# The first three layer norms of a two-block transformer kernel computed by halves of the tokens

## The chip, the cores and the metric

One NeuronCore of one Trainium2 chip runs the whole program; the metric is device microseconds of one execution, lower is better. The engines are TensorE (PE, with PEld for its weight loads), VectorE (DVE), ScalarE (ACT), GpSimd (POOL) and SyncE (SP), which only issues transfers here.

## The reference

x is 512 tokens by 1024 features, fp32. Two blocks run one after the other, each of two layers. Only the first block has the norms of this case:

```python
def layer_norm(x, g, b):
    mu = mean(x, -1); var = mean(square(x - mu), -1)
    return (x - mu) * rsqrt(var + 1e-5) * g + b

for i in range(2):
    mix = s5_mixer(h) if i == 0 else stick_breaking_mixer(h)   # end in h @ w_out, o @ w_o
    h = layer_norm(ALPHA * h + mix, ...)                       # norm 0, norm 2
    h = layer_norm(ALPHA * h + swiglu_ffn(h), ...)             # norm 1, norm 3
```

ALPHA is 4 ** 0.25. swiglu_ffn is (silu(g) * u) @ w_down with (g, u) = split(h @ w_gu), hidden width 2816. The second block (gated attention, a convolutional feed-forward, rms norms 4 to 7) follows and is not changed.

## The kernel before

**Layout.** Features lie on the 128 partitions and tokens on the free axis, so a tensor of 1024 features is 8 chunks of 128x512. `res` (residual) holds h in fp32. Each operand of a dense product is split into a high part rounded to fp32r and a low part, the rest: `xhi`, `xlo` for the input, `whi`, `wlo` for the weights. A product takes three matmuls for each k-chunk: hi*hi, lo*hi, hi*lo.

**Stages.** The program is a list of dense stages in order: glu, ssm_out, gu0, down0, q, k, v, w_o, gu1, down1, ev_u and so on. Weights come in tiles of 128x2048, two buffers (half 0 and half 1) of each of `w_stage`, `w_hi`, `w_lo`. SP loads `w_stage`; ACT casts it to `w_hi` (L1562) once PE has done with the tile before in that buffer; DVE subtracts to make `w_lo` (L2207). ssm_out and w_o have four tiles and 8 output chunks of 24 matmuls each, gathered in banks 0 to 3 of PSUM. In the last pass PE does chunks 4 and 5 from tile half 0 (L975 to L977), then chunks 6 and 7 from tile half 1 (L845 to L847). down0 has one output chunk for each pair of tiles, 66 matmuls of 11 k-chunks a tile. The stage behind a norm (gu0, q, gu1) begins with 48 matmuls of two output chunks on its tile half 0, for each k both chunks, and each k waits for `x_ready` of that k; then 48 on tile half 1.

**Norm n of 0, 1, 2, as it is before.** DVE writes the residual chunk `res` (L2252) and its square (L2263) when PE has done the chunk. POOL sums the chunks and the squares into `acc` (L573) and `acc_sq` (L575), one by one, up to chunk 6, and then makes `w_lo` of tile half 1 of the next stage (L559, `split_last`). PE forms the sums over partitions as matmuls with a matrix of ones: `acc` (L1062), chunk 7 (L1064), `acc_sq` (L1065), the square of chunk 7 (L1067), 512 tokens wide, fp32. ACT squares the mean (L1609), DVE subtracts for the variance (L2336), ACT does Ln and Exp for 1/sqrt (L1611, L1613). Then for each of 8 chunks DVE subtracts the mean (`centre`, L2339) and multiplies (L2350), ACT writes `xhi` (L1619) and `res` (L1620) with gain and bias, and DVE writes `xlo` (L2343), which raises `x_ready`. All engines take their instructions in the order written; all waits are semaphore counts written by hand.

**Halved stages that exist before.** ev_out, cdown0 and od_out (norms 5, 6, 7, rms) already do their last output chunks by halves of the tokens: first tokens 0 to 255 of the last chunks, then tokens 256 to 511 (`halved_units`, `halved_unit`, L857 to L859), with the sums of the first half between (`half_mean_square`, L869, L872). The next stage starts with `first_units_by_halves` (L926 to L928): for each weight tile, first 8 k-chunks of tokens 0 to 255, then of 256 to 511, each waiting for `x_ready` of that k and half; between k 1 and k 2 of the first half stand the sums of the second. There DVE has two operations for a chunk and half, and `w_lo` of tile half 1 is made by POOL.

## Time and profile before

| | |
|---|---|
| median of 3 runs | 2556.41 us (2554.3 to 2556.71) |
| profiled execution, its own time | 2554.76 us |
| span of its trace | 2553.0 us |
| granted TensorE clock, mean | 0.981 |
| busy: PE, DVE, ACT, POOL | 96%, 48%, 32%, 12% |

The time of the execution is 1.76 us more than the span, from the first instruction to the last. A row of the timeline gives start, duration and instruction, and in brackets how long its engine sat idle before it and what ended that. A matmul's recorded duration is longer than the distance to the next one, since matmuls are pipelined; distances between starts are what counts. The granted clock is 1.00 at 2.4 GHz and 0.50 at 1.2 GHz.

### The profile page before, as it was taken

How to read it: one execution, taken by the hardware profiler on the slowest of the kernel's cores; microseconds unless marked ns; L12 is line 12 of the kernel's file. 1: busy time of each engine (PE TensorE's matmuls, PEld its weight loads, DVE VectorE, ACT ScalarE, POOL GpSimd, SP SyncE). 2: the span in 40 equal slices, each digit the busy share in tenths (PEclk: the TensorE clock that was granted, in tenths of full speed). 3: DMA queues.
4: the chain of work that ended last, by engine and by line, in shares of the span. 5: the costliest groups of instructions: out<-in, count | busy, mean ns of one | idle time of the engine just before them, and what ended most of it. 6: DMA issues, size and time to landing. Idle time of an engine off the chain costs nothing.

```text
span 2553.0 us, 32215 instructions
## 1 busy us (share of the span) xinstructions
PE 2459.4 (96%) x12941; PEld 2017.4 (79%) x12941; DVE 1233.3 (48%) x1618; ACT 824.9 (32%) x923; POOL 304.7 (12%) x213
## 2 busy tenths in 40 slices
PE   7699999999999989999989989999999999999999
PEld 6587788887897668888858758888889986988887
DVE  8835433345435564333544464555434445644432
ACT  5422322223225523222243363333323243432222
POOL 6503000004000040000221013000023001100000
PEclk8899999999999989999999989999999999999999
DMA  2432232233320013322342211323233221233232
GB/s 54 92 103 92 83 98 91 77 102 95 99 86 14 11 56 99 99 93 80 91 121 67 67 34 50 108 92 98 85 93 105 83 83 50 83 99 99 84 91 90
DMA packets 254438, 210.30 MB, mean 82 GB/s; under 512 B 7156, under 2 KB 252298, under 8 KB 254250
## 3 DMA queue, kind: packets, MB, share of 16 engines
q1 hardware_dynamic: 250682, 205.99, 26.2%
q8 instruction: 102, 1.67, 0.3%
q0 software_dynamic: 976, 1.74, 0.3%
q10 hardware_dynamic: 2656, 0.72, 0.1%
q14 instruction: 22, 0.18, 0.0%
HBM read 203.97 MB, written 2.10 MB: 81 GB/s over the span
## 4 chain that ended last, share of the span: by engine, by line
PE 89%; DVE 7%; ACT 2%; POOL 1%; issue 1%; DMA 0%; SPq 0%; DVEq 0%; POOLq 0%; ACTq 0%
PE psum L845 14%; PE psum L847 14%; PE psum L846 14%; PE psum L975 9%; PE psum L976 9%; PE psum L977 9%; PE psum L1088 2%; PE psum L1089 2%; PE psum L1090 2%; POOL tmp_a L575 1%; PE psum L1120 1%; PE psum L1138 1%; PE psum L926 1%; PE psum L927 1%; PE psum L928 1%
## 5 line engine op out<-in xcount | busy, mean ns | idle before, releaser
L1562 ACT CAST w_hi<-w_stage 128x2048 fp32r<-128x2048 f32 x209 | 400.4, 1916 | 1341.2 <-PE psum L847 714.5
L2207 DVE TENSOR_TENSOR w_lo<-w_stage,w_hi 128x2048 fp32r<-128x2048 f32 x202 | 473.8, 2345 | 634.5 <-ACT w_hi L1562 634.4
L975 PE MATMUL psum<-x_hi,w_hi 128*128 128x512 f32 x864 | 341.1, 395 | 19.9 <-DVE x_lo L2343 16.1
L845 PE MATMUL psum<-x_hi,w_hi 128*128 128x512 f32 x888 | 345.9, 390 | 0.0
L846 PE MATMUL psum<-x_lo,w_hi 128*128 128x512 f32 x888 | 345.5, 389 | 0.0
L847 PE MATMUL psum<-x_hi,w_lo 128*128 128x512 f32 x888 | 345.5, 389 | 0.0
L976 PE MATMUL psum<-x_lo,w_hi 128*128 128x512 f32 x864 | 339.7, 393 | 0.0
L977 PE MATMUL psum<-x_hi,w_lo 128*128 128x512 f32 x864 | 339.3, 393 | 0.0
L845 PE MATMUL psum<-hidden_hi,w_hi 128*128 128x512 f32 x746 | 291.4, 391 | 0.8 <-DVE w_lo L2207 0.8
L847 PE MATMUL psum<-hidden_hi,w_lo 128*128 128x512 f32 x746 | 290.3, 389 | 0.0
L846 PE MATMUL psum<-hidden_lo,w_hi 128*128 128x512 f32 x746 | 290.2, 389 | 0.0
L975 PEld LDWEIGHTS psum<-x_hi,w_hi 128*128 128x128 f32 x864 | 164.4, 190 | 58.4 <-issue 23.5
L845 PEld LDWEIGHTS psum<-x_hi,w_hi 128*128 128x128 f32 x888 | 166.7, 188 | 35.2 <-issue 0.7
L847 PEld LDWEIGHTS psum<-x_hi,w_lo 128*128 128x128 f32 x888 | 166.7, 188 | 34.7
L846 PEld LDWEIGHTS psum<-x_lo,w_hi 128*128 128x128 f32 x888 | 166.7, 188 | 34.4
L977 PEld LDWEIGHTS psum<-x_hi,w_lo 128*128 128x128 f32 x864 | 164.3, 190 | 34.7
L976 PEld LDWEIGHTS psum<-x_lo,w_hi 128*128 128x128 f32 x864 | 164.5, 190 | 34.0
L845 PEld LDWEIGHTS psum<-hidden_hi,w_hi 128*128 128x128 f32 x746 | 140.0, 188 | 30.8 <-issue 2.1
L846 PEld LDWEIGHTS psum<-hidden_lo,w_hi 128*128 128x128 f32 x746 | 140.0, 188 | 29.5 <-issue 0.5
L847 PEld LDWEIGHTS psum<-hidden_hi,w_lo 128*128 128x128 f32 x746 | 140.0, 188 | 29.2
L565 POOL TENSOR_TENSOR tmp_a<-residual 128x512 f32<-128x512 f32 x4 | 7.2, 1793 | 945.3 <-DVE residual L2252 831.0
L1088 PE MATMUL psum<-w_hi,x_hi 128*128 128x256 f32 x384 | 109.6, 285 | 0.8 <-ACT qk_rstd L1780 0.8
(436 smaller groups left out, 3437.9 us busy)
## 6 DMA issues: line engine op xcount, KB each, us to landing
w_stage<-in_ffn_w_gu_dram SPq DMA_DIRECT2D x44, 1024.0 KB, 5.1
w_stage<-in_ffn_w_down_dram SPq DMA_DIRECT2D x64, 704.0 KB, 4.6
w_stage<-in_ffn_w_gate_dram SPq DMA_DIRECT2D x22, 1024.0 KB, 5.2
w_stage<-in_ffn_w_up_dram SPq DMA_DIRECT2D x22, 1024.0 KB, 5.4
w_stage<-in_sb_w_qkv_dram SPq DMA_DIRECT2D x12, 1024.0 KB, 5.1
w_stage<-in_od_w_in_dram SPq DMA_DIRECT2D x12, 1024.0 KB, 5.3
w_stage<-in_ev_w_in_dram SPq DMA_DIRECT2D x10, 1024.0 KB, 5.1
w_stage<-in_ssm_w_glu_dram SPq DMA_DIRECT2D x8, 1024.0 KB, 5.5
```

The source lines that it names most:

```text
L575: sum_link(nc.gpsimd.tensor_tensor(acc_sq, acc_sq, dev_slot[c], ALU.add))
L845: nc.tensor.matmul(dst, hi, x_hi, start=(start and k == 0), stop=False)
L846: nc.tensor.matmul(dst, hi, x_lo, start=False, stop=False)
L847: mm = nc.tensor.matmul(dst, lo, x_hi, start=False, stop=(stop and k == kn - 1))
L975: nc.tensor.matmul(dst[u], hi, x_hi, start=(k == order[0]), stop=False)
L976: nc.tensor.matmul(dst[u], hi, x_lo, start=False, stop=False)
L977: mm = nc.tensor.matmul(dst[u], lo, x_hi, start=False, stop=(k == order[-1]))
L1088: nc.tensor.matmul(dst, hi, wh[:, k, :], start=(k == 0), stop=False)
L1089: nc.tensor.matmul(dst, hi, wl[:, k, :], start=False, stop=False)
L1090: mm = nc.tensor.matmul(dst, lo, wh[:, k, :], start=False, stop=(k == DC - 1))
L1562: nc.scalar.copy(whi[:, half, :], wst[:, half, :]).then_inc(whi_done, 1)
L2207: V.tensor_tensor(wlo[:, half, :], wst[:, half, :], whi[:, half, :].bitcast(F32), ALU.subtract).then_inc(wlo_done, 1)
```

## The change

Norms 0, 1 and 2 are treated by halves of the tokens. ssm_out, down0 and w_o join the halved stages (chunks 6 and 7 by halves for norms 0 and 2, chunk 7 for norm 1); gu0, q and gu1 start with `first_units_by_halves`. POOL sums only the chunks ahead of the halved ones (to chunk 5, for norm 1 to chunk 6). PE takes the halved chunks and their squares into the sums by matmuls of 256 tokens: three and three for each half (two and two for norm 1), where there were four of 512. ACT and DVE do the norm as 16 steps of 128x256 where there were 8 of 128x512. POOL's `split_last` falls away for these norms; ACT's cast of tile half 1 moves into its norm loop (behind step 9), and DVE makes `w_lo` of it behind its step 10. For norm 1 the cast and subtraction of tile half 0 of the next stage stand behind step 1 too. `xlo` is written by DVE, as before. Norms 3 to 7 keep their work and get new counts.

```diff
-HALVED_LAST = {"ev_out": 2, "cdown0": 1, "od_out": 2}
+HALVED_LAST = {"ssm_out": 2, "down0": 1, "w_o": 2, "ev_out": 2, "cdown0": 1, "od_out": 2}
...
-            return (DC - 1,) if n == 6 else (DC - 2, DC - 1)
+            return (DC - 1,) if n in (1, 6) else (DC - 2, DC - 1)
...
+        mean_half, ln_rstd_half = (bank[5][:, 0:HALF], bank[4][:, HALF:SEQ]), (bank[6][:, 0:HALF], bank[7][:, HALF:SEQ])
...
                 pool.wait_ge(shift_done, n + 1)
-                for c in range(1, DC - 1):
+                for c in range(1, DC - 1 if n == 3 else halved_chunks(n)[0]):
...
-                split_last(n)
+                if n == 3:
+                    split_last(n)
...
                 if h == 0:
                     pe.wait_ge(acc_link, acc_count(n - 1) + 2 * last[0] - 1)
-                else:
+                if n < 3:
+                    nc.tensor.matmul(mean_half[h], ones_mean[:, :], acc[:, tokens], start=True, stop=False)
+                    for c in last:
+                        pe.wait_ge(evac_done, half_done(n, h, c))
+                        mm = nc.tensor.matmul(mean_half[h], ones_mean[:, :], res[:, c, tokens], start=False, stop=(c == last[-1]))
+                    mm.then_inc(ln_sums, 1)
+                    nc.tensor.matmul(ln_rstd_half[h], ones_mean[:, :], acc_sq[:, tokens], start=True, stop=False)
+                    for c in last:
+                        pe.wait_ge(dev_sq, squares_before(n) + last[0] + h * len(last) + (c - last[0]) + 1)
+                        mm = nc.tensor.matmul(ln_rstd_half[h], ones_mean[:, :], dev_slot[c][:, tokens], start=False,
+                                              stop=(c == last[-1]))
+                    mm.then_inc(ln_sums, 1)
+                    return
+                if h == 1:
                     pe.wait_ge(act_link, link_count(n) + 2)
...
                 elif name == "ssm_out":
-                    feature_stage(name, hhi, hlo, lambda k: (hid_ready, DC + k + 1), 0)
-                    norm(0)
+                    feature_stage(name, hhi, hlo, lambda k: (hid_ready, DC + k + 1), 0, norm_out=0)
                 elif name == "gu0":
-                    feature_stage(name, xhi, xlo, lambda k: (x_ready, 1 * DC + k + 1))
+                    feature_stage(name, xhi, xlo, lambda k: (x_ready, x_count(1)), norm_in=0)
...
+            def layer_norm_by_halves(n, affine):
...
+                mean_square_of(0)
+                rstd_of(0)
+                for m in range(2 * DC):
+                    tokens, c = TOKEN_HALVES[m // DC], m % DC
+                    act.wait_ge(ln_n, done + m + 1)
+                    g, b = (prm[:, col + c:col + c + 1] for col in affine)
+                    nc.scalar.activation(xhi[:, c, tokens], res[:, c, tokens], ACT.Identity, bias=b, scale=g).then_inc(ln_hi, 1)
+                    nc.scalar.activation(res[:, c, tokens], res[:, c, tokens], ACT.Identity, bias=b, scale=g).then_inc(ln_a, 1)
+                    if m == 1 and n == 1:
+                        split(st.it0 + st.iters, 0, st.part1 - 1)
+                    if m == 4:
+                        mean_square_of(1)
+                    if m == 5:
+                        rstd_of(1)
+                    if m == DC + 1:
+                        split(st.it0 + st.iters, 1, st.part1)
...
+            def norm_by_halves(n):
...
+                def residual_half(c, h):
...
+                    dve.wait_ge(part_done, parts)
+                    dve.wait_ge(ln_shifted, n * DC + c + 1)
+                    V.scalar_tensor_tensor(res[:, c, tokens], res[:, c, tokens], ALPHA, of[:, tokens], ALU.mult,
+                                           ALU.add).then_inc(evac_done, 1)
+                    dve.wait_ge(evac_done, half_done(n, h, c))
...
+                    V.tensor_tensor(dev_slot[c][:, tokens], res[:, c, tokens], res[:, c, tokens], ALU.mult).then_inc(dev_sq, 1)
...
+                for c in last:
+                    residual_half(c, 0)
+                variance_of(0)
+                centre(0)
+                centre(1)
+                if n != 1:
+                    residual_half(DC - 2, 1)
+                dve.wait_ge(act_link, link_count(n) + 2)
+                for m in range(DC):
+                    scale(m)
+                    if m + 2 < DC:
+                        centre(m + 2)
+                    if m == 1 and n == 1:
+                        split(st.it0 + st.iters, 0)
+                    if m == (2 if n == 1 else 1):
+                        residual_half(DC - 1, 1)
+                    if m > 1:
+                        low_part(m - 2)
+                    if m == 5:
+                        variance_of(1)
+                centre(DC)
+                low_part(DC - 2)
+                centre(DC + 1)
+                low_part(DC - 1)
+                dve.wait_ge(act_link, link_count(n) + 4)
+                for m in range(DC, 2 * DC):
+                    scale(m)
+                    if m + 2 < 2 * DC:
+                        centre(m + 2)
+                    if m > DC + 1:
+                        low_part(m - 2)
+                    if m == DC + 2:
+                        split(st.it0 + st.iters, 1)
+                low_part(2 * DC - 2)
+                low_part(2 * DC - 1)
```

down0 and w_o, q and gu1 are changed like ssm_out and gu0. `variance_of`, `centre`, `scale` and `low_part` are the DVE operations of before on 256 tokens, each with its wait.

## Rows read from the trace of the kernel before

The columns of the waits are: engine and line that waited, what it waited for, us in total, times, longest. Those of a stretch are: its ends, its length, busy us and instructions of PE, PEld, DVE, ACT and POOL, granted clock, DMA share, GB/s.

**Rows 1.** The page: the chain that ended last, share of the span by engine.
```profile
PE 89%; DVE 7%; ACT 2%; POOL 1%; issue 1%; DMA 0%; SPq 0%; DVEq 0%; POOLq 0%; ACTq 0%
```

**Rows 2.** Waits of PE over the whole span.
```profile
PE psum L975 <- DVE x_lo L2343: 16.1, 3, 5.5
...
PE psum L1062 <- POOL tmp_a L575: 5.7, 2, 2.9
```

**Rows 3.** Timeline of PE around the first norm: start us, us, instruction, idle before.
```profile
249.25 0.39 PE L847 MATMUL psum<-hidden_hi,w_lo 128*128 128x512 f32 x1
...
249.93 0.39 PE L847 MATMUL psum<-hidden_hi,w_lo 128*128 128x512 f32 x1
...
253.15 1.13 PE L1062 MATMUL psum<-tmp_a,ones_mean 128*128 128x512 f32 x2 [2.83 <-POOL tmp_a L575]
...
262.19 0.77 PE L975 MATMUL psum<-x_hi,w_hi 128*128 128x512 f32 x1 [5.34 <-DVE x_lo L2343]
...
276.01 0.39 PE L845 MATMUL psum<-x_hi,w_hi 128*128 128x512 f32 x1
```

**Rows 4.** Timeline of PE around the second and third norm.
```profile
625.56 0.39 PE L847 MATMUL psum<-hidden_hi,w_lo 128*128 128x512 f32 x1
...
648.49 0.39 PE L845 MATMUL psum<-x_hi,w_hi 128*128 128x512 f32 x1
...
938.25 0.39 PE L847 MATMUL psum<-hidden_hi,w_lo 128*128 128x512 f32 x1
...
967.02 0.39 PE L845 MATMUL psum<-x_hi,w_hi 128*128 128x512 f32 x1
```

**Rows 5.** Stretches behind idle time of PE: busy us (count), granted clock, DMA.
```profile
262.20:268.30 6.10, 6.10 (x14) 4.75 (x15) 6.10 (x11) 5.02 (x7) 0.00 (x0) 0.50 0.01 3
...
941.50:948.20 6.70, 6.68 (x8) 2.52 (x8) 0.00 (x0) 0.60 (x1) 4.50 (x1) 0.55 0.00 0
```

**Rows 6.** Timeline of PE in a stage already halved, ev_out into conv0.
```profile
1569.92 0.28 PE L857 MATMUL psum<-x_hi,w_hi 128*128 128x256 f32 x1
...
1577.47 0.60 PE L869 MATMUL psum<-tmp_a,ones_mean 128*128 128x256 f32 x2
...
1578.88 0.28 PE L858 MATMUL psum<-x_lo,w_hi 128*128 128x256 f32 x1
...
1608.20 0.40 PE L975 MATMUL psum<-x_hi,w_hi 128*128 128x512 f32 x1
```

**Rows 7.** Timeline of DVE: first norm, and two half-width steps of ev_out.
```profile
242.50 3.37 DVE L2207 TENSOR_TENSOR w_lo<-w_stage,w_hi 128x2048 fp32r<-128x2048 f32 x1
...
256.96 0.69 DVE L2336 TENSOR_TENSOR tmp_c<-psum,tmp_c 128x512 f32<-128x512 f32 x1 [4.98 <-PE psum L1067]
...
259.07 0.69 DVE L2350 TENSOR_TENSOR residual<-residual,psum 128x512 f32<-128x512 f32 x1 [0.23 <-ACT psum L1613]
...
263.16 0.69 DVE L2343 TENSOR_TENSOR x_lo<-residual,x_hi 128x512 fp32r<-128x512 f32 x1
...
264.95 0.69 DVE L2343 TENSOR_TENSOR x_lo<-residual,x_hi 128x512 fp32r<-128x512 f32 x1
...
1582.02 0.41 DVE L2476 TENSOR_TENSOR residual<-residual,psum 128x256 f32<-128x256 f32 x1
...
1582.35 0.48 DVE L2485 SCALAR_TENSOR_TENSOR psum<-residual,params,psum 128x256 f32<-128x256 f32 x1
```

**Rows 8.** Timeline of POOL: its last sum of chunk 5, first norm.
```profile
248.79 1.28 POOL L575 TENSOR_TENSOR tmp_a<-tmp_a,squares 128x512 f32<-128x512 f32 x1
```

**Rows 9.** Groups by form: line, engine, shapes, count | busy, mean ns | idle.
```profile
L1562 ACT CAST w_hi<-w_stage 128x2048 fp32r<-128x2048 f32 x209 | 400.4, 1916 | 1341.2 <-PE psum L847 714.5 <-PE psum L977 526.3 <-PE psum L1090 80.8
...
L1620 ACT ACTIVATE residual<-residual,params 128x512 f32<-128x512 f32 x32 | 25.7, 804 | 1.1 <-DVE residual L2350 1.1
...
L1646 ACT ACTIVATE squares<-residual 128x256 f32<-128x256 f32 x10 | 4.2, 419 | 16.2 <-DVE residual L2476 16.2
...
L2207 DVE TENSOR_TENSOR w_lo<-w_stage,w_hi 128x2048 fp32r<-128x2048 f32 x202 | 473.8, 2345 | 634.5 <-ACT w_hi L1562 634.4
```

More of the change, by code:

```diff
@@ L1626, in layer_norm, with mean_square_of, rstd_of @@
                         nc.scalar.activation(sq[:, (c - 1) % 2, :], res[:, c - 1, :], ACT.Square).then_inc(ln_sq, 1)
+            def layer_norm_by_halves(n, affine):
+                st, last = ST[norm_stage[n]], halved_chunks(n)
+                done = n * 2 * DC
+                def mean_square_of(h):
+                    act.wait_ge(ln_sums, 4 * n + 2 * h + 1)
+                    nc.scalar.activation(mean_sq[:, TOKEN_HALVES[h]], mean_half[h], ACT.Square).then_inc(ln_m2, 1)
+                def rstd_of(h):
+                    tokens = TOKEN_HALVES[h]
+                    act.wait_ge(ln_var, 2 * n + h + 1)
+                    nc.scalar.activation(rstd_ln[:, tokens], variance[:, tokens], ACT.Ln, bias=eps_ln[:, 0:1]).then_inc(act_link, 1)
+                    act.wait_ge(act_link, link_count(n) + 2 * h + 1)
+                    nc.scalar.activation(ln_rstd_half[h], rstd_ln[:, tokens], ACT.Exp, scale=-0.5).then_inc(act_link, 1)
+                mean_square_of(0)
[14 more added lines that the diff above has]
+                        split(st.it0 + st.iters, 1, st.part1)
             def rms_norm(n):
@@ L2317, in down_stage @@
                     shift(n)
-                    for c in range(looped, DC):
+                    for c in range(looped, DC if n == 3 else DC - 1):
                         unit(c - c % 2, c % 2, c < DC - 1, True)
@@ L2355, in norm, with variance_of, centre, scale @@
                 pass_split(n)
-                if n < 3:
-                    low(DC - 1)
+            def norm_by_halves(n):
+                st, last = ST[norm_stage[n]], halved_chunks(n)
+                before = n * 2 * DC
+                def residual_half(c, h):
+                    tokens = TOKEN_HALVES[h]
+                    if n == 1:
+                        parts, of = st.part1 - 2 * (1 - h), bank[1 + h]
+                    else:
+                        parts, of = st.part1 - 4 + 2 * h + (c - last[0]) + 1, bank[2 + c - last[0]]
+                    dve.wait_ge(part_done, parts)
[3 more added lines that the diff above has]
+                    dve.wait_ge(evac_done, half_done(n, h, c))
+                    if c == DC - 1:
+                        dve.wait_ge(acc_link, acc_count(n - 1) + 3)
+                    V.tensor_tensor(dev_slot[c][:, tokens], res[:, c, tokens], res[:, c, tokens], ALU.mult).then_inc(dev_sq, 1)
+                def variance_of(h):
+                    tokens = TOKEN_HALVES[h]
+                    dve.wait_ge(ln_m2, 2 * n + h + 1)
+                    dve.wait_ge(ln_sums, 4 * n + 2 * h + 2)
+                    V.tensor_tensor(variance[:, tokens], ln_rstd_half[h], mean_sq[:, tokens], ALU.subtract).then_inc(ln_var, 1)
+                def centre(m):
+                    tokens, c = TOKEN_HALVES[m // DC], m % DC
+                    V.tensor_tensor(res[:, c, tokens], res[:, c, tokens], mean_half[m // DC], ALU.subtract).then_inc(ln_xc, 1)
+                def scale(m):
+                    tokens, c = TOKEN_HALVES[m // DC], m % DC
+                    dve.wait_ge(ln_xc, before + m + 1)
+                    V.tensor_tensor(res[:, c, tokens], res[:, c, tokens], ln_rstd_half[m // DC], ALU.mult).then_inc(ln_n, 1)
+                def low_part(m):
+                    tokens, c = TOKEN_HALVES[m // DC], m % DC
+                    dve.wait_ge(ln_a, before + m + 1)
+                    V.tensor_tensor(xlo[:, c, tokens], res[:, c, tokens], xhi[:, c, tokens].bitcast(F32),
+                                    ALU.subtract).then_inc(x_ready, 1)
+                for c in last:
[5 more added lines that the diff above has]
+                    residual_half(DC - 2, 1)
+                dve.wait_ge(act_link, link_count(n) + 2)
+                for m in range(DC):
[25 more added lines that the diff above has]
+                low_part(2 * DC - 1)
@@ L2740, in _ @@
                     down_stage(name, 1)
-                    norm(1)
+                    norm_by_halves(1)
                 elif name == "q":
```

81 lines of the change are left out of this document (37 added, 44 removed).

## Prediction

> **What bounds the kernel now.** I read the page's chain first: PE sets the end for 89% of the span [rows 1], so time is won or lost only where PE stands idle, runs at half clock, or does more matmuls. The list of PE's waits then says where: three waits for `xlo`, 16.1 us, one behind each of norms 0, 1 and 2, and two for POOL's sums, 5.7 us, at norms 0 and 2 [rows 2]. The timelines of PE give the whole price of a norm: from the start of the last dense matmul before it to the start of the 49th behind it, less 49 matmuls at their distance. That distance is (249.93 - 249.25) / 3 = 0.227 us [rows 3], so 49 are 11.1 us. Norm 0 costs 276.01 - 249.93 - 11.1 = 15.0 us [rows 3]; norm 1 costs 648.49 - 625.56 - 11.1 = 11.8 and norm 2 costs 967.02 - 938.25 - 11.1 = 17.7 [rows 4]. Together 44.5 us. In these lie spells of half clock: behind the 5.34 us of idle time of norm 0 the clock is 0.50 for 6.1 us [rows 3, 5], and 6.7 us after 941.5, behind the second wait for POOL, it is 0.55 [rows 5].
>
> The question is what the same stretches cost by halves. Each engine takes its instructions in order, so I lay them out, with these prices.
>
> **Prices of the pieces.**
> - A dense matmul of 256 tokens: (1577.47 - 1569.92) / 63 = 0.120 us [rows 6], against 0.113 for half of 0.227.
> - A sum of 256 tokens in fp32: three of them and the first step behind took 1578.88 - 1577.47 = 1.41 us [rows 6]; less one dense matmul that is 0.37 each and 0.18 once. Six are 2.4 us, four 1.7.
> - DVE at 128x256: 1582.35 - 1582.02 = 0.33 us from start to start [rows 7]. At 512 a loop step of three operations took 264.95 - 263.16 = 1.79, or 0.60 each [rows 7]. So a step of centre, scale, low is 1.0 us by halves, 16 steps 16 us against 14.3.
> - ACT at 128x256 with gain and bias is in no row. It lies between 0.42, a Square of that shape, and 0.80, the same operation at 512 [rows 9]. I take the middle, 0.61 or 0.50 from start to start (0.09 overlap as on DVE); the low end gives 0.42 from start to start and the high end 0.71. A step has two, so 1.0 us: ACT and DVE are level.
> - Cast of a weight tile on ACT 1.92, subtraction on DVE 2.35 [rows 9], less where nothing contends; I use 2.25.
> - From the variance to the first scale took 259.07 - 256.96 = 2.1 us at 512 [rows 7]; at 256 I take 1.4 (between 1.05, half, and 2.1).
>
> The Trainium skill ("VectorE: DVE Perf Modes", section on the TRN2 errata for SBUF-source operations) says that each instruction pays a fixed cost and advises tiles of 512 elements or more. The trace agrees, 0.33 against half of 0.60; without that cost 16 steps would be 14.3 us, with it 16. It speaks against this change, by 1.7 us a norm on DVE.
>
> **Norm 0, laid out.** Chunk 6 starts at 249.93 - 47 x 0.227 = 239.28. Its first half is 24 x 0.120 = 2.88 us, to 242.16, chunk 7's to 245.04. For the second half of chunk 6 PE needs the bank evacuated, but DVE is in a weight subtraction from 242.50 to 245.87 [rows 7]. Evacuation ends at 246.29: PE waits 1.3. Fifteen matmuls later, at 248.1, it wants POOL's sums to chunk 5; the last of them ends at 248.79 + 1.28 = 250.07 [rows 8]. PE waits 2.0. POOL's list ahead of that is the one of before, only chunk 6 (two sums) and its weight subtraction go. Sums to 252.5, the other 33 matmuls to 256.5.
>
> DVE starts the variance at 252.6 and scale 0 at 254.6, behind the evacuation and square of chunk 6's second half. Behind scale 1 it stands before the evacuation of chunk 7's second half, which PE finishes at 256.5; then come both operations, scale 2, centre 4, and only then low 0, done at 258.6. PE waits 2.1. From there `xlo` comes at 1.0 us a step, where PE needs 6 x 0.120 = 0.72. PE does k 0 and k 1, then the second sums (2.4), which cover some steps; DVE waits 1.3 for them before its second variance. Step 7 is there at 266.7, step 8 at 269.0.
>
> **The wait that decides.** Behind low 8 DVE must subtract the weights of tile half 1. ACT casts them only behind its step 9: cast from 269.05 to 270.96, DVE idle 2.1 us, subtraction to 273.2. Queued behind it are scale 11 and low 9, and PE's k 9 waits for low 9: done at 274.25, PE idle 4.5 us at k 9. The cast and POOL's L559 were in nobody's way before; POOL took that subtraction in 4.5 us beside the norm. Low 10 to 15 follow to 279.2, k 15 ends at 279.9, and tile half 1 takes 96 x 0.120 = 11.5: 291.45. Before it was 276.01 + 48 x 0.227 = 286.9 [rows 3]. Norm 0: **+4.6 us**.
>
> **Norm 1.** Chunk 7 starts at 625.56 - 65 x 0.227 = 610.8. First half 66 x 0.120, to 618.8, 12 matmuls, four sums at 620.2 (POOL has nothing left there), second half done at 628.3. Scale 0 at 623.4, scale 1, and now the cast of tile half 0, which ACT reaches at 625.8: DVE idle 3.1, subtraction 627.8 to 630.0. Then scale 2, chunk 7's evacuation and square, low 0 at 631.8; PE idle 3.5. Step 8 at 641.6, the second cast and subtraction as in norm 0 (PE idle 4.5), low 15 at 651.8, end of tile half 1 at 664.0. Before: 648.49 + 10.9 = 659.4 [rows 4]. **+4.7 us**.
>
> **Norm 2** has the list of norm 0; its end lies 291.45 - 249.93 = 41.5 behind the last dense matmul: 979.8, against 967.02 + 10.9 = 977.9 [rows 4]. **+1.9 us**, better than norm 0 because the sums of before ran at half clock there. Sum at full clock: **+11.2 us**.
>
> SP's load of the next tile for half 1 can start at 273.2, when `w_stage` is free, and its cast is wanted at 291, so it stays hidden (before, the free point was POOL's and DVE's mark behind the norm loop). The three norms are the only places changed; the new counts of norms 3 to 7 move nothing.
>
> **The clock.** Half clock stands behind the wait of 5.34 us [rows 3, 5] and behind the second wait for POOL, of 2.9 us [rows 2]: eight passes of the sums in 6.7 us there [rows 5]. Behind the first, of 2.83 us, it does not: two passes in 1.13 us [rows 3]. The new wait at k 9 is 4.5 us, so I take half clock behind it for 5.1 us, 24 dense matmuls at 0.213. They need 1.28 us a k against DVE's 1.0, and what PE falls behind is partly caught up at 0.72: +1.6 us for each norm, +4.9. If the clock falls at the waits of 2 us as well, the sums take double, which delays DVE too: then the norms cost 11.7, 10.4 and 9.0 more than before, +31.
>
> The Trainium skill ("TensorE: Matmul & The Clock Gate", Part 1) says that idleness brings half clock and sustained work releases it. The trace agrees [rows 5]; by the rule the case with fallen clock is the likelier, as taken.
>
> **The forecast.** 11.2 + 4.9 = 16.1 us more. The sum is made against the profiled execution, 2554.76 us (span 2553.0 and 1.76 around it): 2570.9. The runs' median is 1.65 above it, so 2572.4.
>
> **Rivals.**
> 1. The same without fallen clock, +11.2: 2567.6. For it: the waits are shorter than 5.34. Chance 0.22; the forecast 0.42.
> 2. Half clock at the short waits too, +31: 2587. Chance 0.13. For it the 2.86 us row, against it the 2.83 us one.
> 3. The casts and subtractions of tile half 1 cost PE nothing, because the second half of x is not waited for: then my layout gives +1.0, +1.1, -1.7, together +0.4: 2556.8, no difference. Against it stands the order on DVE. Chance 0.12.
> 4. **Faster:** the layer norm by halves costs PE what the rms norm by halves costs in ev_out and conv0. There it took 1608.20 - 1569.92 = 38.3 us [rows 6] for 144 matmuls of 512, 32.7 us: 5.6 lost. With three more sums a half, 2.2 us, that is 7.8 a norm, 23.4 for three against 44.5: -21.1, 2535.3. For it: PE had hardly a wait for `xlo` there. Against it: DVE had two operations a step and no weight subtraction in the norm. It decides where a norm loses less than (44.5 - 5.1) / 3 = 13.1 us; my layout has 19.6 in norms 0 and 2, 16.5 in norm 1. Chance 0.11.
>
> 0.2% is 5.1 us, about what a measurement of this kernel can tell from no change. Slower: forecast, rivals 1 and 2, 0.77. Same: 0.12. Faster: 0.11. The likeliest case alone has 2563 to 2579: the low end is ACT at 0.42 and DVE at 0.30 a step, which takes 4.5 off the +11.2, with part of the clock loss; the high end is ACT at 0.54 and DVE at 0.36, +3.5, and a little more clock. The range for 8 in 10 goes from rival 3, 2556, to 2583, which leaves out rival 4 and most of rival 2.
>
> **What the profile after would show.** PE idle about 4.5 us once in each of gu0, q and gu1, inside the first tile, waiting for `xlo`, with DVE's `w_lo` before it, itself waiting for ACT's `w_hi`: the step that carries the result. PE waiting some 2 us for POOL's `tmp_a` in ssm_out and w_o, and 2 to 3.5 us before the first matmul of the next stage. `xlo` steps 1.0 us apart. Half clock behind the long wait. ACT's operations at 0.6 us or less. The prediction is wrong if the three stretches, from the last 512-wide matmul to the end of the next stage's first two tiles, together are not longer than before (in norm 0: 36.9 us from 249.93), or if PE reaches the second half without waiting.

## The result, and the profile after

The changed kernel takes 2575.59 us in the median (2573.39 to 2578.39, 4 runs) where the kernel before took 2555.51 on the same chip: a ratio of 1.0079, 95% interval 1.0063 to 1.0095. It is slower by 0.8%. The forecast was 2572.4, range 2556 to 2583. The profiled execution took 2577.76 us (span 2575.9), 23.0 more than the one of before.

The list of PE's waits after the change, over the whole span. The two lines of [rows 2] that it replaces are gone.

```profile
PE psum L946 <- DVE x_lo L2438: 24.6, 9, 4.3
...
PE psum L875 <- POOL tmp_a L581: 3.2, 2, 1.6
...
PE psum L864 <- DVE residual L2413: 2.1, 2, 1.1
...
PE psum L864 <- DVE w_lo L2255: 1.4, 2, 1.0
```

Nine waits for `xlo` where there were three, 24.6 us instead of 16.1. PE's timeline at norm 0, after the change (columns as in [rows 3]):

```profile
243.81 0.28 PE L864 MATMUL psum<-hidden_hi,w_hi 128*128 128x256 f32 x1
...
250.79 0.39 PE L864 MATMUL psum<-hidden_hi,w_hi 128*128 128x256 f32 x1 [1.07 <-DVE residual L2413]
...
254.42 0.70 PE L875 MATMUL psum<-tmp_a,ones_mean 128*128 128x256 f32 x2 [1.57 <-POOL tmp_a L581]
...
263.30 0.36 PE L946 MATMUL psum<-x_hi,w_hi 128*128 128x256 f32 x1 [2.06 <-DVE x_lo L2438]
...
265.01 0.60 PE L875 MATMUL psum<-tmp_a,ones_mean 128*128 128x256 f32 x2
...
274.10 0.39 PE L946 MATMUL psum<-x_hi,w_hi 128*128 128x256 f32 x1 [1.34 <-DVE x_lo L2438]
...
279.34 0.58 PE L946 MATMUL psum<-x_hi,w_hi 128*128 128x256 f32 x1 [4.26 <-DVE x_lo L2438]
...
297.37 0.40 PE L995 MATMUL psum<-x_hi,w_hi 128*128 128x512 f32 x1
```

Four small waits, the last of them (1.34 us) at k 8, then the long one at k 9. What made it stands in the timelines of ACT and DVE in the same stretch:

```profile
274.07 1.89 ACT L1579 CAST w_hi<-w_stage 128x2048 fp32r<-128x2048 f32 x1
...
273.63 0.42 DVE L2438 TENSOR_TENSOR x_lo<-residual,x_hi 128x256 fp32r<-128x256 f32 x1
275.99 2.29 DVE L2255 TENSOR_TENSOR w_lo<-w_stage,w_hi 128x2048 fp32r<-128x2048 f32 x1 [1.95 <-ACT w_hi L1579]
...
278.87 0.42 DVE L2438 TENSOR_TENSOR x_lo<-residual,x_hi 128x256 fp32r<-128x256 f32 x1
```

Low 8 ends at 274.05 and low 9 starts at 278.87: between them DVE is idle 1.95 us for ACT's cast, then subtracts weights for 2.2 and does a scale and a centre.

The yardstick below is a stretch that holds a whole norm: from the first half-width matmul of the stage ahead of it to the first 512-wide matmul of the third weight tile behind it. After the change the three are 297.37 - 243.81 = 53.56, 57.66 and 53.43 us. Before, the same work began 47, 65 and 47 matmuls ahead of the start rows and ended 48 behind the end rows of [rows 3, 4]: 47.61, 48.54 and 50.31, together 146.46. The windows of the kernel after, cut at these points, say where all the time went (columns as in [rows 5]):

```profile
0.00:243.80 243.80, 207.24 (x1921) 179.58 (x1922) 157.09 (x342) 85.76 (x99) 85.11 (x82) 0.90 0.32 85
243.80:297.40 53.60, 43.19 (x314) 40.97 (x313) 32.76 (x67) 26.72 (x44) 10.18 (x6) 0.94 0.18 60
297.40:621.30 323.90, 323.49 (x1426) 267.17 (x1425) 133.65 (x120) 76.14 (x55) 21.73 (x11) 1.00 0.30 93
621.30:679.00 57.70, 47.40 (x342) 45.57 (x341) 31.23 (x63) 26.35 (x42) 5.42 (x4) 0.91 0.26 83
679.00:947.20 268.20, 268.20 (x1540) 209.28 (x1539) 135.45 (x195) 96.43 (x111) 11.59 (x6) 1.00 0.16 52
947.20:1000.70 53.50, 43.09 (x314) 40.85 (x313) 32.79 (x67) 26.72 (x44) 10.20 (x6) 0.94 0.18 60
1000.70:2575.90 1575.20, 1542.45 (x7586) 1272.42 (x7584) 724.66 (x854) 499.81 (x585) 140.65 (x93) 0.99 0.28 85
```

Before, cut in the same way:

```profile
0.00:239.30 239.30, 200.85 (x1922) 173.77 (x1923) 157.08 (x342) 85.63 (x99) 85.15 (x82) 0.94 0.32 86
...
286.90:610.80 323.90, 323.48 (x1425) 267.27 (x1424) 132.01 (x117) 76.36 (x55) 21.74 (x11) 1.00 0.30 93
...
659.40:927.60 268.20, 268.20 (x1540) 209.28 (x1539) 134.96 (x194) 96.64 (x111) 11.62 (x6) 1.00 0.16 52
...
977.90:2553.00 1575.10, 1542.20 (x7585) 1272.30 (x7583) 723.02 (x851) 500.88 (x585) 140.72 (x93) 0.99 0.28 85
```

The parts between and behind the norms are equal to 0.1 us. The norms cost 18.2 us more (6.0, 9.1 and 3.1; 146.46 became 164.65). The start-up, which the change does not touch, took 4.5 us more in this execution, at a mean granted clock of 0.90 instead of 0.94. In the profiled executions of all kernels below it ends anywhere between 239.27 and 244.28 us. So a single time is uncertain by some 5 us, and the sum of the three stretches is the sharper measure of a norm. It comes from one execution of each kernel and has a spread of its own: norm 1, which e5_front and e6_order below leave as it is, took 57.58 and 58.85 us in them against 57.66 here.

### The profile page after: what moved, and what is told of

Same layout as the page of the kernel before. It is cut to its first block, busy times and chain, and to the rows that moved or that the text cites. A ratio compares the mean times of both kernels' runs of the same rounds, so it can differ in the third digit from the quotient of the medians.

```text
span 2575.9 us, 33325 instructions
## 1 busy us (share of the span) xinstructions
PE 2475.0 (96%) x13431; PEld 2055.8 (80%) x13431; DVE 1247.6 (48%) x1703; ACT 837.9 (33%) x980; POOL 284.9 (11%) x206
## 4 chain that ended last, share of the span: by engine, by line
PE 88%; DVE 7%; ACT 2%; POOL 1%; issue 1%; DMA 0%; SPq 0%; DVEq 0%; POOLq 0%; ACTq 0%
PE psum L852 14%; PE psum L853 14%; PE psum L854 14%; PE psum L995 8%; PE psum L997 8%; PE psum L996 8%; PE psum L1108 2%; PE psum L1109 2%; PE psum L1110 2%; PE psum L946 2%; PE psum L947 1%; PE psum L948 1%; ACT w_hi L1579 1%; DVE w_lo L2255 1%; POOL tmp_a L581 1%
## 5 line engine op out<-in xcount | busy, mean ns | idle before, releaser
L852 PE MATMUL psum<-x_hi,w_hi 128*128 128x512 f32 x840 | 327.2, 390 | 0.0
L853 PE MATMUL psum<-x_lo,w_hi 128*128 128x512 f32 x840 | 326.9, 389 | 0.0
L854 PE MATMUL psum<-x_hi,w_lo 128*128 128x512 f32 x840 | 326.8, 389 | 0.0
L995 PE MATMUL psum<-x_hi,w_hi 128*128 128x512 f32 x816 | 318.6, 390 | 3.7 <-DVE x_lo L2580 3.7
L997 PE MATMUL psum<-x_hi,w_lo 128*128 128x512 f32 x816 | 318.2, 390 | 0.0
L996 PE MATMUL psum<-x_lo,w_hi 128*128 128x512 f32 x816 | 318.0, 390 | 0.0
L852 PE MATMUL psum<-hidden_hi,w_hi 128*128 128x512 f32 x692 | 270.4, 391 | 0.8 <-DVE w_lo L2255 0.8
L854 PE MATMUL psum<-hidden_hi,w_lo 128*128 128x512 f32 x692 | 269.3, 389 | 0.0
L853 PE MATMUL psum<-hidden_lo,w_hi 128*128 128x512 f32 x692 | 269.3, 389 | 0.0
L852 PEld LDWEIGHTS psum<-x_hi,w_hi 128*128 128x128 f32 x840 | 157.7, 188 | 33.4 <-issue 0.7
L854 PEld LDWEIGHTS psum<-x_hi,w_lo 128*128 128x128 f32 x840 | 157.7, 188 | 32.9
L853 PEld LDWEIGHTS psum<-x_lo,w_hi 128*128 128x128 f32 x840 | 157.7, 188 | 32.5
L995 PEld LDWEIGHTS psum<-x_hi,w_hi 128*128 128x128 f32 x816 | 153.6, 188 | 36.3 <-issue 4.7
L997 PEld LDWEIGHTS psum<-x_hi,w_lo 128*128 128x128 f32 x816 | 153.5, 188 | 32.1
L996 PEld LDWEIGHTS psum<-x_lo,w_hi 128*128 128x128 f32 x816 | 153.6, 188 | 31.6
L946 PE MATMUL psum<-x_hi,w_hi 128*128 128x256 f32 x384 | 116.4, 303 | 26.1 <-DVE x_lo L2438 24.6
```

What stands on the lines that cost most here:

```text
L852: nc.tensor.matmul(dst, hi, x_hi, start=(start and k == 0), stop=False)
L853: nc.tensor.matmul(dst, hi, x_lo, start=False, stop=False)
L854: mm = nc.tensor.matmul(dst, lo, x_hi, start=False, stop=(stop and k == kn - 1))
L946: nc.tensor.matmul(dst, hi, xh[:, k, tokens], start=(k == 0), stop=False)
L995: nc.tensor.matmul(dst[u], hi, x_hi, start=(k == order[0]), stop=False)
L996: nc.tensor.matmul(dst[u], hi, x_lo, start=False, stop=False)
```

## The experiments

Eleven further kernels ran. The results in one table; the change of the stretches is against 146.46, that of the time is the ratio less 1, times 2555.

| kernel | stretches, us | sum | against before | ratio (95% interval) | as time |
|---|---|---|---|---|---|
| changed kernel | 53.56, 57.66, 53.43 | 164.65 | +18.2 | 1.0079 (1.0063 to 1.0095) | +20.2 |
| e1_late | 52.04, 58.13, 54.70 | 164.87 | +18.4 | 1.0072 (1.0058 to 1.0085) | +18.4 |
| e2_pool | 56.84, 59.35, 55.24 | 171.43 | +25.0 | 1.0097 (1.0082 to 1.0112) | +24.8 |
| e3_early | 50.85, 53.91, 50.86 | 155.62 | +9.2 | 1.0033 (1.0020 to 1.0046) | +8.4 |
| e4_fill | 52.75, 57.15, 54.10 | 164.00 | +17.5 | 1.0074 (1.0061 to 1.0087) | +18.9 |
| e5_front | 51.55, 57.58, 53.09 | 162.22 | +15.8 | 1.0064 (1.0050 to 1.0078) | +16.4 |
| e6_order | 53.28, 58.85, 52.81 | 164.94 | +18.5 | 1.0069 (1.0056 to 1.0083) | +17.6 |
| e7_cast0 | 53.47, 53.98, 53.49 | 160.94 | +14.5 | 1.0068 (1.0054 to 1.0082) | +17.4 |
| e8_all | 48.52, 52.27, 48.51 | 149.30 | +2.8 | 1.0012 (1.0003 to 1.0021) | +3.1 |
| e9_whi_first | 50.48, 53.03, 50.72 | 154.23 | +7.8 | 1.0037 (1.0023 to 1.0051) | +9.5 |
| e10_last | 45.84, 48.96, 45.85 | 140.65 | -5.8 | 0.9973 (0.9964 to 0.9983) | -6.9 |
| e11_cast_mid | 46.37, 50.11, 46.36 | 142.84 | -3.6 | 0.9988 (0.9979 to 0.9997) | -3.1 |

The two measures agree within 3 us everywhere, so what a kernel gains or loses it does in these stretches.

**e1_late: the splits of tile half 1 behind the last step.**

```diff
 # ACT, layer_norm_by_halves: out of the loop
-                    if m == DC + 1:
-                        split(st.it0 + st.iters, 1, st.part1)
+                split(st.it0 + st.iters, 1, st.part1)
 # DVE, norm_by_halves
-                    if m == DC + 2:
-                        split(st.it0 + st.iters, 1)
                 low_part(2 * DC - 2)
                 low_part(2 * DC - 1)
+                split(st.it0 + st.iters, 1)
```

> ACT's cast of tile half 1 and DVE's subtraction both stand behind step 15 of the norm, in all three norms; nothing else differs from the changed kernel. Theory (the cast and the subtraction cost PE because they stand ahead of low 9): the 4.3 us waits of PE for x_lo at k 9 vanish and low 15 is done at 281.1 in norm 0 instead of 284.1, but the cast then starts at 280.7, the subtraction ends at 284.8, and PE, through with k 15 at 281.9, waits some 2.9 us for w_lo: next 512-wide matmul at 296.3 instead of 297.4, so 1.1 us a norm less, and 2 us less where the clock then stays at 1.00: in all 3 to 6 us less than the changed kernel (2575.6). Rival (the second half of x is not what PE waits for, the splits are costless once they are behind it): the whole wait and its clock go, 5.9 us a norm, 17.7 in all, 2558. Rival (where they stand makes no difference, only their length counts): no change.

Median 2574.91 us, ratio 1.0072. The wait at k 9 is gone in all three norms and a wait for `w_lo` stands ahead of tile half 1 instead. PE in e1_late, norm 0, at k 9 and at the start of tile half 1:

```profile
271.52 0.38 PE L946 MATMUL psum<-x_hi,w_hi 128*128 128x256 f32 x1
...
280.67 0.38 PE L946 MATMUL psum<-x_hi,w_hi 128*128 128x256 f32 x1 [2.68 <-DVE w_lo L2254]
```

The long wait was for the queue position of the split, as the theory says, and moving it to the end only makes PE wait for the split itself: 2.7 us against the 2.9 expected, and 1.5 us won in norm 0. In norms 1 and 2 the stretches grew by 0.5 and 1.3, so the 3 to 6 us expected in all did not come. That is clock: behind the same wait of 2.7 us PE took 11.6 us for tile half 1 in norm 0, 13.1 in norm 1 and 14.3 in norm 2, at a granted clock of 1.00, 0.87 and 0.79. Taken whole, this kernel can't be told from the changed one.

**e2_pool: POOL makes that `w_lo` again. ACT's cast stays behind its step 9.**

```diff
-                if n == 3:
-                    split_last(n)
+                split_last(n)
...
 # DVE: the split behind step 10 goes
                 low_part(2 * DC - 1)
+                pass_split(n)
```

> POOL makes w_lo of tile half 1 again in the three norms, as in the kernel before; ACT's cast stays behind its step 9; DVE passes the count behind low 15. Theory, DVE's queue alone: DVE has no hole at step 10 beyond ACT's cast, so of the 4.3 us wait at k 9 some 1.5 us are left, at k 10, low 15 comes at 282.4 instead of 284.1, and the next 512-wide matmul 2.8 us earlier than in the changed kernel in norm 0; 8 us less in three norms, 2567, somewhat less with the half clock gone. Rival (contention): DVE's operations with two operands in SBUF take 1.05 us instead of 0.42 while POOL runs its sums (squares of 256 tokens at 250.77 and 252.19 in the profile after), so about four lows beside POOL's 4.5 us take 0.7 us more each, and POOL itself takes longer: the gain is eaten, 0 to 2 us in all. Rival (the wait at k 9 was no more than a shift of work): no change and PE waits the same 4.3 us elsewhere.

Median 2581.24 us, ratio 1.0097: 6.8 us more in the stretches than the changed kernel, worse than even the contention rival gave. POOL, then DVE in e2_pool:

```profile
274.98 4.50 POOL L565 TENSOR_TENSOR w_lo<-w_stage,w_hi 128x2048 fp32r<-128x2048 f32 x1 [23.16 <-ACT w_hi L1578]
```

```profile
275.87 3.90 DVE L2437 TENSOR_TENSOR x_lo<-residual,x_hi 128x256 fp32r<-128x256 f32 x1 [1.28 <-ACT residual L1665]
279.69 0.41 DVE L2432 TENSOR_TENSOR residual<-residual,psum 128x256 f32<-128x256 f32 x1
```

One `low_part`, 0.42 us elsewhere, takes 3.90 us: it starts inside POOL's subtraction and ends at 279.77, 0.3 us behind POOL's end at 279.48. It is not slowed in proportion, it stands until POOL has finished, and the whole norm behind it. Norms 1 and 2 show the same, with 3.91 us each. The four lows of 0.7 us more each in the expectation had the wrong form; it is one low that pays for nearly all of POOL's instruction. The Trainium skill ("SBUF — State Buffer", section "SBUF: two separate sides") says that a DVE operation with two SBUF inputs and a GpSimd operation take a common port pair by turns, whole instruction by whole instruction. The trace agrees, by the end of the low 0.3 us behind POOL's. Not all of the 6.8 us is this: ahead of k 8, where the kernels do the same work, e2_pool lost 1.4 us in norm 0 and 1.1 in norm 1 to half clock around the second sums. From k 8 on it lost 1.8, 0.6 and 1.8 us, together 4.2.

Before the change POOL's subtraction ran from 253.17 to 257.68 in norm 0, ahead of the first low (261.35). That place is gone: in the changed kernel PE uses the old weights of tile half 1 until its matmul at 260.95, and low 0 starts at 262.73. That an earlier cast would not have helped POOL is argued from these times; no such kernel was run.

**e3_early: the splits where ACT and DVE wait for the second sums anyway.**

```diff
 # ACT
                     if m == 4:
+                        split(st.it0 + st.iters, 1, st.part1)
                         mean_square_of(1)
 # DVE
                     if m == 5:
+                        split(st.it0 + st.iters, 1)
                         variance_of(1)
 # the splits behind ACT's step 9 and DVE's step 10 go
```

> ACT's cast of tile half 1 stands ahead of its square of the second mean (behind step 4), DVE's subtraction ahead of its second variance (behind step 5): both fall into the time in which ACT (1.1 us) and DVE (1.7 us) wait for PE's second sums. Theory: the 4.3 us wait at k 9 goes in all three norms, the second variance comes 0.5 to 0.9 us later, low 15 is done about 280.7 in norm 0 instead of 284.1, and the next 512-wide matmul comes 4.4 us earlier; 13 us less in all, about 2562, still 6 to 7 us above the kernel before. Rival (PE needs a total of DVE work, its place is indifferent): the wait moves to k 4 or k 8 with the same 4 us, 0 to 2 us less. Rival (layer norm by halves loses only through this wait and its clock): 18 us less, level with the kernel before at 2556.

Median 2564.49 us, ratio 1.0033: 9.0 us less in the stretches than the changed kernel (13 expected), 11.1 less in time. The largest of the three waits for `xlo` in each norm is gone. Ahead of it two things happen that the expectation did not have. PE and DVE in e3_early, norm 0, and then norm 2:

```profile
261.45 0.36 PE L946 MATMUL psum<-x_hi,w_hi 128*128 128x256 f32 x1 [2.06 <-DVE x_lo L2437]
...
263.83 1.05 PE L875 MATMUL psum<-tmp_a,ones_mean 128*128 128x256 f32 x2
...
266.93 0.47 PE L946 MATMUL psum<-x_hi,w_hi 128*128 128x256 f32 x1
...
268.92 0.39 PE L946 MATMUL psum<-x_hi,w_hi 128*128 128x256 f32 x1 [0.22 <-DVE x_lo L2437]
```

```profile
267.79 0.42 DVE L2423 TENSOR_TENSOR tmp_c<-psum,tmp_c 128x256 f32<-128x256 f32 x1
```

```profile
958.38 0.36 PE L946 MATMUL psum<-x_hi,w_hi 128*128 128x256 f32 x1 [2.06 <-DVE x_lo L2437]
...
962.51 0.47 PE L946 MATMUL psum<-x_hi,w_hi 128*128 128x256 f32 x1
...
965.86 0.38 PE L946 MATMUL psum<-x_hi,w_hi 128*128 128x256 f32 x1 [1.57 <-DVE x_lo L2437]
```

First, behind the same wait of 2.06 us the same 12 matmuls and six sums take 5.5 us in norm 0, at half clock, and 4.1 in norm 2. The difference costs nothing here: PE only waits 0.22 us at k 4 instead of 1.57, and k 8 starts 32.0 us behind the start of the stretch in both, which take 50.85 and 50.86 us. Second, DVE's place was not free. The subtraction waits 1.28 us for ACT's cast, and the second variance (L2423) starts 25.8 us behind the start of the stretch in both norms, against 24.1 in the changed kernel: 1.75 later, where 0.5 to 0.9 was expected. This is what holds k 4 and k 8. Low 15 of norm 0 is done 1.9 us earlier in the stretch than in the changed kernel, where 3.4 was expected. About 1 us of the 1.5 missing is the late variance; the rest was not followed. So the rival is right in part: some of the long wait moved to k 4.

**e4_fill: 33 matmuls of no use ahead of the wait at k 9.**

```diff
+                            if n < 3 and pair == 0 and h == 1 and k == 0:
+                                for _ in range(33):
+                                    nc.tensor.matmul(bank[5][:, 0:HALF], whi[:, 0, 0:P], xh[:, 0, 0:HALF], start=True, stop=True)
```

> Ahead of PE's wait at k 9 of the second half, in the three norms, PE does 33 additional matmuls of 256 tokens into a bank that nothing reads any more (4.0 us of the 4.3 us wait). No other work changes. Theory (half clock behind the wait costs 1.6 us or more a norm): granted clock 1.00 behind k 9 in all three norms, next 512-wide matmul 1.5 to 2 us earlier in each, 5 us less in all, 2571. Rival 1 of the prediction (the clock costs nothing, DVE sets the pace there): the clock is 1.00 and the time is that of the changed kernel. Rival: the filler only delays PE where the wait is shorter than 4 us; some us more.

Median 2574.46 us, ratio 1.0074. From k 9 to the end of the stretch (PE and the windows of e4_fill, norm 0):

```profile
276.90 0.39 PE L946 MATMUL psum<-x_hi,w_hi 128*128 128x256 f32 x1 [0.30 <-DVE x_lo L2441]
...
294.13 0.40 PE L998 MATMUL psum<-x_hi,w_hi 128*128 128x512 f32 x1
```

```profile
276.90:294.10 17.20, 17.16 (x138) 16.75 (x139) 6.44 (x14) 8.56 (x13) 0.00 (x0) 1.00 0.38 123
```

and the same stretch of the changed kernel:

```profile
279.30:297.30 18.00, 17.96 (x138) 17.96 (x139) 6.46 (x13) 8.59 (x13) 0.00 (x0) 0.91 0.36 118
```

At full clock it takes 17.23 us, in all three norms. In the changed kernel it took 18.03, 18.56 and 17.90. Half clock behind the long wait cost 0.8, 1.3 and 0.7 us, together 2.8. The forecast had 1.6 for each and this expectation 1.5 to 2. Of these 2.8 us the sum shows 0.6, because ahead of k 9 norms 1 and 2 were 0.8 and 1.3 us longer this time (the part that the filler does not touch; the second sums and first matmuls ran at half clock there).

**e5_front, e6_order, e7_cast0: three smaller places, each alone** (the last two edits in short form).

```diff
 # e5_front, DVE out_stage, and norm_by_halves for norms 0 and 2
-                    elif c % 2 == 1 and c < DC - 1:
+                    elif c % 2 == 1 and (c < 5 or n not in (0, 2)):
                         split(st.it0 + 1 + c // 4, c % 4 // 2)
...
                 for c in last:
                     residual_half(c, 0)
+                if n != 1:
+                    split(st.it0 + st.iters, 0)
                 variance_of(0)
 # e6_order, DVE, norms 0 and 2
-                    if m == 1: residual_half(DC - 1, 1)
+                    if m == 2: low_part(0); residual_half(DC - 1, 1); low_part(1)
 # e7_cast0, norm 1: ACT, then DVE
-                    if m == 1: split(half 0)
+                    if m == 0: split(half 0)
-                    if m == 1: split(half 0)
-                    if m == 2: residual_half(DC - 1, 1); low_part(0)
+                    if m == 2: low_part(0); split(half 0); residual_half(DC - 1, 1); low_part(1)
```

> For norms 0 and 2 DVE's subtraction for tile half 0 of the next stage stands behind the two evacuations of the first halves (chunks 6 and 7) instead of ahead of them; all else as in the changed kernel. Theory: PE's 1.07 us wait for the bank goes, and POOL's sum beside that subtraction (3.21 us long there, 1.3 to 1.7 elsewhere) is shortened, so that the sums of the first half end about 1.4 us earlier in norm 0 (256.93 before) and everything behind them too: 53.56 becomes about 52.1 us from the first half-width matmul to the next 512-wide one, the same in norm 2 (53.43); 3 us less in all. Rival: POOL's last sums are beside the moved subtraction now and end as late as before; PE only waits 1.07 longer at the sums, no gain. Norm 1 stays at 57.7.

51.55 us in norm 0, 2.0 less than in the changed kernel (1.4 expected), 0.3 less in norm 2. PE's wait for the bank is gone and the one for POOL is 1.00 us instead of 1.57, in both. The rival is out in norm 0; in norm 2 the first matmul of the next stage came 1.9 us earlier too, but the k 9 matmul only 0.6. Between them PE ran at half clock behind the wait of 2.06 us: the second sums took 3.0 us instead of 2.4. In total time none of e5_front, e6_order and e7_cast0 can be told from the changed kernel, so all three are judged by their stretches.

> For norms 0 and 2 low 0 stands ahead of, and low 1 directly behind, the evacuation and square of the second half of chunk 7, which itself stands behind step 2 instead of step 1. Theory (PE's 2.06 us wait ahead of the next stage is for an xlo that stands behind an evacuation that itself waits for PE): the wait shrinks to about 0.3 us, the second sums start 1.6 us earlier, DVE's idle 1.7 us ahead of its second variance goes, and the next 512-wide matmul comes 1.6 us earlier in norms 0 and 2; 3 us less in all. The wait of 4.3 us at k 9 stays as long as it is. Rival (a chain elsewhere sets the end): the time moves into the wait at k 9 or at k 8 and the stretch stays 53.5 us.

The theory was right on the wait and wrong on the gain. PE's wait ahead of the next stage fell from 2.06 to 0.51 us and k 9 came 34.1 us behind the start of the stretch instead of 35.5. But the stretch is only 0.3 us shorter in norm 0. PE, then the windows, of e6_order:

```profile
275.47 0.58 PE L946 MATMUL psum<-x_hi,w_hi 128*128 128x256 f32 x1 [4.26 <-DVE x_lo L2438]
...
294.66 0.40 PE L995 MATMUL psum<-x_hi,w_hi 128*128 128x512 f32 x1
```

```profile
275.00:281.00 6.00, 5.53 (x26) 5.53 (x27) 4.60 (x14) 5.98 (x11) 0.00 (x0) 0.50 0.56 178
```

From k 9 on it took 19.2 us where full clock takes 17.2: six microseconds at half clock, where the changed kernel had a mean of 0.66 over 4.7. Of the 1.4 us won 1.2 went to the clock. Norm 2 gained 0.6. Norm 1, which the edit leaves alone, took 1.2 more in this execution, so the sum shows no gain.

> Norm 1 alone: ACT casts tile half 0 of the next stage behind its step 0 instead of step 1, and DVE's order is step 2, low 0, the subtraction, the evacuation of chunk 7's second half, low 1. Theory: the subtraction ends 1.0 us earlier and low 0 and low 1 no longer stand behind it with the evacuation and a step between, so that the first matmul of q comes some 19.5 us behind the first half-width matmul of down0 instead of 22.55, PE's wait of 3.66 us falls to about 0.6, and the clock does not fall behind it (the four second sums then take 1.7 us, not 2.3): the stretch of norm 1 is 53.3 to 54.7 us instead of 57.66, 3 to 4.4 us less in all. Rival (the clock does not hang on this wait): 3 us less at most, sums still at half clock. Rival (PE's pace in norm 1 is set by DVE behind the first matmul anyway): under 1 us.

Norm 1 takes 53.98 us instead of 57.66, as the theory gave. The wait of 3.66 us is one of 0.79, now for `w_lo` of tile half 0, and the first matmul of q comes 19.7 us behind the start.

**e8_all: e3_early and the three together.**

> The early place of both halves' cast and subtraction (as in the kernel whose stretches were 50.85, 53.91 and 50.86 us), and the three edits of the other kernels of this call together. Theory (the losses lie one behind another on one chain and add): 50.85 - 1.4 - 1.6 = 47.8 us in norm 0, 49.9 in norm 1, 47.8 in norm 2, sum 145.5 against 146.4 in the kernel before: about 2554.5, no difference that can be measured from before. Rival (they overlap: DVE's sum of work from scale 0 on, 19.4 us without any idle time, is the floor): 49 us in norm 0, the sum 150, 2559. Rival (the half clock goes as well everywhere): 143, 2552.

Median 2559.04 us, ratio 1.0012; 48.52, 52.27, 48.51, the sum 149.3, which is the rival's 150. The gains do not add. PE in e8_all, norm 0, at k 4:

```profile
268.75 0.39 PE L946 MATMUL psum<-x_hi,w_hi 128*128 128x256 f32 x1 [2.56 <-DVE x_lo L2437]
```

The first matmul of the next stage comes 3.5 us earlier than in e3_early, in norms 0 and 2, but k 8 only 2.3. DVE waits 1.61 us for the cast (1.28 in e3_early) and then subtracts, and PE stands 2.56 us at k 4, where it stood 1.57 in norm 2 of e3_early, at full clock. The split stood on the path in its new place already there, and it shows more now that PE gets to it earlier. So the next kernels took it out of the path.

**e9_whi_first: e1_late, and PE's order within tile half 1.**

```diff
                     if pair == 1 and n < 3:
+                        pe.wait_ge(whi_done, st.it0 * 2 + 2)
...                      # all k: w_hi with xh and xl, 512 tokens wide
+                        pe.wait_ge(wlo_done, st.it0 * 2 + 2)
...                      # all k: w_lo with xh
```

> The kernel with cast and subtraction behind step 15 (stretches 52.04, 58.13 and 54.70 us, PE waiting 2.7 us for w_lo of tile half 1), and one more edit: PE takes tile half 1 of the stage behind a norm as 512-wide matmuls, first the 32 products with w_hi, then the 16 with w_lo. Theory (PE then waits for ACT's cast alone, and the subtraction lies beside 7 us of matmuls): PE starts tile half 1 when the cast ends, 278.3 in norm 0 instead of 280.7, and takes 48 x 0.227 = 10.9 us for it instead of 11.5: 3 us less a norm, sum of the stretches 156 instead of 164.9, 9 us less in all, about 2566. Rival (the wait for w_lo hides another one, for the bank's evacuation or for the next tile's weights, whose load now starts later): the time comes back as a wait for w_hi or the DMA in the tile behind, under 3 us less in all.

Median 2565.89 us, ratio 1.0037; the sum 154.2. PE waits 0.35 us for `w_hi` where it waited 2.68 for `w_lo`, and no wait for `w_lo` follows. PE in e9_whi_first, norm 0:

```profile
283.72 0.50 PE L946 MATMUL psum<-x_hi,w_hi 128*128 128x512 f32 x1 [0.35 <-ACT w_hi L1595]
```

**e10_last and e11_cast_mid: everything together, the cast last or in the middle.** e10_last is e9_whi_first with the edits of e5, e6 and e7; e11_cast_mid differs from it only in ACT's cast, which stands ahead of `mean_square_of(1)`.

> All edits together with both splits of tile half 1 behind step 15: front (subtraction for tile half 0 behind the first evacuations), order (low 0 ahead of and low 1 behind chunk 7's second evacuation), norm 1's cast behind step 0, and PE's tile half 1 with the w_hi products first. Theory: no split stands in the chain of steps any more, ACT does its 1.0 us a step from the second variance on, low 15 is done some 31 us behind the first half-width matmul, PE starts tile half 1 at the end of the cast: stretches of 45 to 46 us in norms 0 and 2 and 49 in norm 1, sum 140 against 146.4 in the kernel before: 2549 to 2550, faster than before by 0.2%. Rival (half clock behind short waits takes its share, 0.7 to 1.3 us a norm): sum 143, 2552, no difference that can be measured. Rival (layer norm by halves has no more to give than 48.5 us a stretch, the one with everything early): 2558.

> As the kernel before it in this call, but ACT casts tile half 1 ahead of its square of the second mean (behind step 4). Theory (ACT is the bound of the steps, and 1.9 us of cast among them moves low 15 by what ACT does not idle there, 1 to 1.9 us, where behind step 15 it costs PE only what outlasts the last products, 0.9 us): 1 us a norm more than the kernel with the cast last, sum 143, 2553. Rival (ACT's idle time at the second sums covers the cast wholly): 1 us a norm less than with the cast last.

e10_last: median 2548.98 us, ratio 0.9973 (0.9964 to 0.9983); the stretches 45.84, 48.96 and 45.85, sum 140.65 where 140 was expected. It is faster than the kernel before, by 0.27%. e11_cast_mid: 2551.35, ratio 0.9988, 2.2 us more in the stretches (3 expected). The ratios of these two kernels overlap at the edge of their intervals; the stretches tell them apart in all three norms. PE's waits in e10_last, whole span:

```profile
PE psum L962 <- DVE x_lo L2453: 5.4, 6, 1.3
...
PE psum L875 <- POOL tmp_a L581: 2.0, 2, 1.0
...
PE psum L946 <- ACT w_hi L1595: 1.1, 3, 0.4
```

Waits for `xlo` fell from 24.6 us to 5.4, a third of the 16.1 of [rows 2].

## Why the prediction was right, point by point

- **The bound, and the sum.** Right. The norms cost 18.2 us more, 16.1 was forecast; the rest of the 20.2 us is within the uncertainty of the ratio and the start-up's spread. Two errors cancel in part here. The clock cost 4.2 us (2.8 behind k 9 and 1.4 in norm 1) where 4.9 stood. So the layout at full clock, +11.2, was some 2.8 us short, an estimate from 18.2 - 4.2: 0.6 in each of norms 0 and 2 and 1.7 in norm 1.
- **Prices.** DVE's step of three operations took 1.0 us, as laid out. ACT's two-operand form at 128x256, of which no row existed, took 0.60 us and 0.50 from start to start, the value taken.
- **Norm 0, laid out.** Waits of 1.07, 1.57, 2.06 and 4.26 us against 1.3, 2.0, 2.1 and 4.5. The stretch grew by 6.0 us where 4.6 + 1.6 stood. Of these, 0.8 is clock, so the nearness of the sum is in part luck: the layout was 0.6 us short and the clock 0.8 too dear.
- **Norm 2.** +3.1 us against 1.9 + 1.6.
- **Norm 1.** Mis-sized: +9.1 us against 4.7 + 1.6. The wait ahead of q was 3.66 us as laid out (3.5). Two things were left out. PE waits 0.95 us at 626.38 for `w_lo` of the unit's second tile, because PE is through with the unit's first tile in 4.1 us (621.32 to 625.43) and DVE's subtraction of 2.77 us, begun at 623.46, is not. And the clock fell behind the 3.66 us wait: the first 12 matmuls of q took 2.35 us instead of the 1.71 of norm 0, and the four sums 2.28 instead of the 1.54 of the first four, 1.4 us in all. No run took the wait of 0.95 us away. e7_cast0 took the one of 3.66 away and with it 3.7 us of the stretch. The two waits in the changed kernel:

```profile
626.38 0.36 PE L864 MATMUL psum<-hidden_hi,w_hi 128*128 128x256 f32 x1 [0.95 <-DVE w_lo L2255]
...
643.87 0.36 PE L946 MATMUL psum<-x_hi,w_hi 128*128 128x256 f32 x1 [3.66 <-DVE x_lo L2438]
```

- **The wait that decides.** Shown. Its place and makers are in the timelines. With the splits moved (e3_early) 9.0 us went, and with them out of the path altogether (e9_whi_first against the changed kernel) 10.4, of which 48 matmuls of 512 for 96 of 256 are at most 0.6 a norm. Rival 3, that they cost nothing, is out. But the wait could not be had back by giving the subtraction to POOL, as "POOL took that subtraction in 4.5 us beside the norm" suggested: e2_pool lost 6.8 us, 4.2 of them behind k 8, where POOL holds DVE.
- **The clock.** Right in kind, too large behind k 9: 2.8 us for 4.9. The balance came elsewhere, 1.4 behind norm 1's other wait. Neither rival 1 (none) nor rival 2 (at every short wait) holds.
- **Rival 4, faster.** By the forecast's measure, the stretch less 144 matmuls (162 in norm 1) at 0.227 us, the changed kernel loses 20.9, 20.9 and 20.7 us a norm, far above the 13.1 at which this rival would decide. e10_last goes part of the way once the splits, the low parts and the order of PE's products are arranged for it: stretches 7.7, 8.7 and 7.6 us shorter than the changed kernel's. By the same measure it loses 13.2, 12.2 and 13.2 us a norm, which is still far from this rival's 7.8. Against the kernel before, norm 0 gains 1.8 us, norm 2 4.5, norm 1 nothing (+0.4).

## What to carry to other kernels

When a step is cut in halves so that PE can start sooner, list what else stands in the queues of the engines that feed it. One weight split between two steps cost more than the halving gave, and the best of the places tried was behind the last step, with PE's products reordered so that its result is wanted last. Before moving work to a place where an engine idles, count everything that must fit there: in e3_early DVE idled 1.7 us, the subtraction and its wait for the cast took 3.5, and PE stood at k 4 for it. And before half clock is called a cost, look whether a wait behind it shrinks by as much, as at k 4 in norm 0 of e3_early.
